# Dense projection weights laid out on the host as 96 contiguous quarters

## What is computed

```python
# block 1
u = jnp.einsum('bsd,de->bse', h, w_in[layer])          # 2048 -> 6752 columns
q, k, v, z_attn, q_idx, k_idx, w_idx, z_ssd, xbc, dt_raw = _split_cols(u, IN_WIDTHS)
...                                                    # rope, top-k attention, state space mixer
sub = jnp.einsum('bse,ed->bsd', mixed, w_out[layer])   # 2048 -> 2048
h = _layer_norm(DEEPNORM_ALPHA * h + sub, ln_g[layer], ln_b[layer])
# block 2
mod_shared = jax.nn.silu(c) @ w_mod + b_mod            # one row, 2048 -> 12288
h = rms_norm(x, norm1_g[l]) * (1.0 + scale1) + shift1
proj = h @ w_in[l]                                     # 2048 -> 2560
...                                                    # gated unit, stick-breaking attention
x = x + gate1 * (y @ w_out[l])                         # 1024 -> 2048
m = hierarchical_moe(...)                              # 32 experts, two for each token
x = x + gate2 * m
```

## Time and profile before

| | us |
|---|---|
| median of 3 runs | 1999.33 |
| lowest and highest run | 1998.57, 2000.62 |
| the profiled execution | 2000.42 |
| its span on the core | 1998.6 |

### The profile page before, as it was taken

The page is one execution under the profiler, slowest core; times in us unless marked ns, Lnnn a source line. Parts: engine busy times, 40 slices in busy tenths (PEclk is TensorE's granted clock), DMA queues, the critical chain, the costliest instruction groups (busy, mean ns, idle before and its releaser), DMA issues.

```text
span 1998.6 us, 23417 instructions
## 1 busy us (share of the span) xinstructions
PE 1860.2 (93%) x9558; PEld 1370.9 (69%) x9558; DVE 1067.0 (53%) x1551; ACT 315.2 (16%) x602; POOL 178.5 (9%) x190
## 2 busy tenths in 40 slices
PE   8999999999999999999999999999959988788876
PEld 3788988888787555888888888557845554444443
DVE  3766677544687555767774764435463332232222
ACT  0111221221300232000340122411310000000000
POOL 0000041000000000000000000000002211111211
PEclk9999999999999999999999999999969999999999
DMA  9554543222224437668545651244299999999996
GB/s 354 184 187 154 167 122 94 65 80 63 85 85 158 179 129 281 230 243 294 173 165 211 252 180 64 66 161 169 91 386 395 410 398 406 412 403 403 413 420 241
DMA packets 153225, 448.37 MB, mean 224 GB/s; under 512 B 19446, under 2 KB 118108, under 8 KB 126748
## 3 DMA queue, kind: packets, MB, share of 16 engines
q1 hardware_dynamic: 122012, 305.92, 40.2%
q0 software_dynamic: 24288, 118.32, 17.0%
q10 hardware_dynamic: 6816, 22.60, 3.2%
HBM read 440.42 MB, written 26.28 MB: 234 GB/s over the span
## 4 chain that ended last, share of the span: by engine, by line
PE 39%; DMA 20%; DVE 2%; issue 1%; ACT 0%; POOL 0%; POOLq 0%; SPq 0%; DVEq 0%; ACTq 0%
PE bank L1167 16%; DMA RW<-in_gate_up 9%; PE bank L1196 7%; DMA RG<-in_down 5%; PE bank L1106 4%; DMA RA<-xn_d,dt_ 3%; PE bank L1363 3%; PE bank L1374 2%; DMA RM<-in_down 2%; PE bank L1111 2%; DMA out<-RA,dt_ 1%; PE bank L919 1%; PE bank L992 1%; DVE RG L1958 1%; DMA RG<-in_w_mod 1%
## 5 line engine op out<-in xcount | busy, mean ns | idle before, releaser
L1167 PE MATMUL bank<-RW,RX 128*128 128x256 f32 x1344 | 300.3, 380 | 2.6 <-PE bank L1167 2.0
L1167 PEld LDWEIGHTS bank<-RW,RX 128*128 128x128 f32 x1344 | 253.7, 190 | 44.4 <-issue 10.6
L1958 DVE SCALAR_TENSOR_TENSOR RG<-RG,ccol 128x2048 f32<-128x2048 f32 x90 | 211.6, 2351 | 92.5 <-DMA RG<-in_w_mod 85.8
L1167 PE MATMUL bank<-RW,RM 128*128 128x256 f32 x1024 | 229.3, 380 | 1.5 <-PE bank L1167 0.9
L1167 PEld LDWEIGHTS bank<-RW,RM 128*128 128x128 f32 x1024 | 193.6, 190 | 31.8 <-issue 4.8
L1949 DVE TENSOR_TENSOR RW<-RW 128x2048 f32<-128x2048 f32 (+1 forms) x72 | 160.4, 2233 | 88.8 <-PE bank L1167 66.1
L1434 ACT ACTIVATE RA<-bank 128x512 f32<-128x512 f32 (+4 forms) x160 | 81.1, 540 | 559.2 <-PE bank L1167 246.9
L2879 DVE TENSOR_TENSOR RA<-RA,bank 128x128 f32<-128x128 f32 x34 | 9.8, 288 | 277.9 <-ACT RA L1918 277.7
L837 POOL DMA_DIRECT2D RG<-in_w_mod x96 | 51.4, 536 | 987.7 <-DVE RG L1958 602.0
L1111 PE MATMUL bank<-RX,RW 128*128 128x512 f32 x256 | 114.8, 593 | 2.1 <-ACT RA L1434 1.3
L1363 PE MATMUL bank<-RX,RG 128*64 128x256 f32 x768 | 90.6, 393 | 19.8 <-DMA RX<-in_gate_up 17.1
(11 more groups left out here) (294 smaller groups left out, 2462.9 us busy)
## 6 DMA issues: line engine op xcount, KB each, us to landing
RG<-in_w_mod POOLq DMA_DIRECT2D x96, 1024.0 KB, 6.2
RW<-in_w_in SPq DMA_DIRECT2D x71, 1024.0 KB, 5.4
RX<-in_gate_up SPq DMA_DIRECT2D x22, 2048.0 KB
RW<-in_gate_up SPq DMA_DIRECT2D x22, 2048.0 KB, 39.9
RG<-in_down SPq DMA_DIRECT2D x11, 2048.0 KB, 40.8
RM<-in_down SPq DMA_DIRECT2D x11, 2048.0 KB, 41.5
RM<-in_gate_up SPq DMA_DIRECT2D x10, 2048.0 KB
RH<-in_gate_up SPq DMA_DIRECT2D x10, 2048.0 KB
```

Of the source, the lines that this page charges most:

```text
L1167: ins = nc.tensor.matmul(bk[:, part], x, y, start=name not in ("M2", "M3") and k + j == 0, stop=k == half - 1, skip_group_check=True)
L1958: st.do(v.scalar_tensor_tensor(out=dst, in0=x, scalar=sc, in1=y, op0=op0, op1=op1), s, n)
```

## The change

The host cuts the weights into the 96 quarters that SP loads outside the kind "small" and stacks them as `in_quarters`, in the order of their loads, each as 128 partitions by 8 by 256. SP then reads a quarter as one run of 8 KB for each partition. The first quarter is still loaded in two halves (4 KB a partition each). An out2 quarter becomes one transfer in place of two, and its slot's count goes up by 16 in place of 32. The kind "small" is loaded as before. Nothing else in the program is different: the bytes, the slots, the order of the loads and the waits in front of them stay.

```diff
--- before.py
+++ after.py
@@ -379,13 +379,13 @@
                 return order
             return [(h, n if slots[2 * h] < slots[2 * h + 1] else 1 - n) for h, n in order]
 
-        loads, load_of, release_of = [], {}, {}
+        loads, load_of, release_of, laid_out = [], {}, {}, []
         landed = [0, 0, 0, 0]
         slots_in_turn = [0, 1, 2, 3]
         for c, ch in enumerate(chunks):
             for q in loading(c, slots_in_turn[len(loads):len(loads) + len(quarters(c))]):
                 s = slots_in_turn[len(loads)]
-                landed[s] += 32 if ch[0] in ("small", "out2") else 16
+                landed[s] += 32 if ch[0] == "small" else 16
                 load_of[c, q] = (s, landed[s])
                 loads.append((c, q))
             for q in releases(c):
@@ -716,23 +716,17 @@
                 if n >= 4:
 
                     sp.wait_ge(slot_free, n - 3)
-                if w.tensor.name == a["w_in_2"].tensor.name:
-                    rows = w.rearrange("(p k) n -> p k n", k=KD)
-                else:
+                if kind == "small":
                     rows = w.rearrange("(k p) n -> p k n", p=P)
-                if kind == "small":
                     sp.dma_start(W[:, s, :, 0:80], rows[:, 8 * h:8 * h + 8, C_KI:C_KI + 80]).then_inc(w_landed[s], 16)
                     sp.dma_start(W[:, s, :, 80:96], rows[:, 8 * h:8 * h + 8, C_DT:C_DT + 16]).then_inc(w_landed[s], 16)
-                elif kind == "out2":
-                    for part in range(2):
-                        at = 4 * (1 - part)
-                        sp.dma_start(W[:, s, 4 * part:4 * part + 4, :], rows[:, at:at + 4, col + 256 * half:col + 256 * half + 256]).then_inc(w_landed[s], 16)
                 else:
-                    at = 8 * (1 - h) if kind == "out" else 8 * h
+                    laid_out.append((w.tensor.name, kind, h, col + 256 * half))
+                    piece = a["quarters"][len(laid_out) - 1]
                     early = 4 if n == 0 else 0
                     if early:
-                        sp.dma_start(W[:, s, 0:early, :], rows[:, 0:early, col:col + 256]).then_inc(sem("x_first"), 16)
-                    sp.dma_start(W[:, s, early:, :], rows[:, at + early:at + 8, col + 256 * half:col + 256 * half + 256]).then_inc(w_landed[s], 16)
+                        sp.dma_start(W[:, s, 0:early, :], piece[:, 0:early, :]).then_inc(sem("x_first"), 16)
+                    sp.dma_start(W[:, s, early:, :], piece[:, early:, :]).then_inc(w_landed[s], 16)
                 n += 1
                 if (c, q) == (first["out2"] + 1, (0, 1)):
 
@@ -2971,6 +2965,18 @@
                         dve.wait_ge(sem(f"y_added{u}"), i * 32 + (8 * NST + 16 * (w // 2)))
                         dve.wait_ge(sem(f"wd_landed{u}"), i * 32 + 16 * (w // 2 + 1))
                         take_y(u, WDX[u][:, 0:1])
+    return laid_out
+
+
+def lay_quarter(inputs, name, kind, h, col):
+
+    w = inputs[name[3:]][0]
+    if kind == "out2":
+        return w.reshape(2, 4, P, -1)[::-1, :, :, col:col + 256].reshape(8, P, 256).transpose(1, 0, 2)
+    if name == "in_w_in_2":
+        return w.reshape(P, KD, -1)[:, 8 * h:8 * h + 8, col:col + 256]
+    at = 8 * (1 - h) if kind == "out" else 8 * h
+    return w.reshape(KD, P, -1)[at:at + 8, :, col:col + 256].transpose(1, 0, 2)
 
 
 _INS = ["x", "w_in", "w_out", "conv_w", "conv_b", "dt_bias", "a_log", "d_skip", "ssd_norm_w", "ln_g", "ln_b", "c_2",
@@ -3000,6 +3006,8 @@
     arrays["in_const"] = CONST
     args["const"] = nc.dram_tensor("in_const", CONST.shape, F32, kind="ExternalInput").ap()
     out = nc.dram_tensor("out_0", (1, S, D), F32, kind="ExternalOutput").ap()
-    program(nc, args, out)
+    args["quarters"] = nc.dram_tensor("in_quarters", (96, P, 8, 256), F32, kind="ExternalInput").ap()
+    laid_out = program(nc, args, out)
+    arrays["in_quarters"] = np.stack([lay_quarter(inputs, *piece) for piece in laid_out])
     r = run(nc, [arrays], core_ids=[0])
     return r.results[0]["out_0"]
```

## The result

| | before | changed |
|---|---|---|
| median of 9 runs each, us | 1999.46 | 2006.32 |
| lowest and highest | 1998.57, 2005.72 | 2002.14, 2012.13 |
| the profiled execution | 2000.42 | 2007.78 |
| its span | 1998.6 | 2006.1 |

The changed kernel is slower: ratio 1.0026, 95% interval 1.0016 to 1.0036, that is 3 to 7 us. The forecast was 1998.2 in a range of 1994.5 to 2002.0, with a chance of 0.09 for slower by over 0.2%.

The account below looks back on a forecast made before the run. PE was taken to bound the dense part, expert-weight transfers the expert part. Start -2.5, mod sums +1.4, rest 0 gave -1.1: 1999.3 from the profiled 2000.42, 1998.2 for the median, range 1994.5 to 2002.0.

Parts of the forecast that it names:

- What bounds the kernel: Whole kernel: dense part at PE's pace, expert part at its weights' pace; quicker quarters worth nothing on the path.
- The start: Before PE's first matmul: half quarter and x's first part land together near 7.0; gain 2.5 us, bounds 0 to 2.8.
- the bare sum: At the first matmul: 2.7 + 3.7 + 0.6 = 7.0 us, before 0.3 was taken off the gain for the fit.
- The w_mod pieces: At the mod sums at 835 and 936: pieces land later beside quarters, costing 0.7 us each, 1.4 together.
- the pair itself gets faster: Quarter and w_mod piece before a mod sum: 420 in place of 394 GB/s, piece landing at 933.7 to 934.3.
- the 1.7 us of delay: At a mod sum: piece ends with the pair's last byte, at 935.3 by today's speed, 1.7 us later.
- Rival 1: At the three mod sums: w_mod loses more than the pair gains, 1.7 at each that waits; +2.2, 2001.5 us; chance 0.17.
- Rival 2: At start and sums: nothing moves, since shares ignore run length or long runs are cut again; 1999.3 us; chance 0.14.
- rival 3: Start gives 2.8 and both mod sums' waits vanish, 2.9: clearly faster by 5.7, 1993.6 us; chance 0.14.
- its reserve: At the last mod sum: VectorE done at 1175.14, PE comes at 1178.24; 3.1 us, holding two rounds of 0.7.
- It piles up in VectorE's order: Where further pieces wait in VectorE's order: delay could pile up and the slower case pass +4 us; chance 0.09 beyond that.
- The forecast's own upper end: Whole kernel: top of the forecast's own 1996.5 to 2000, from start 1.5 to 2.8, sums 0 to 3.4 against it.

Follow-up runs that it names:

- out-old kernel: The changed kernel, but the 16 quarters of kind out loaded from w_out in runs of 1 KB as before; 1999.28 us, ratio 0.9982.

## Why the prediction was wrong, point by point

**What bounds the kernel**: right. The dense part is bound by PE, the expert part did not change, the quicker quarters gave nothing on the path, and only the start and the mod sums moved. The out-old kernel shows it for the other 80 quarters: -1.4 us, all of it from the start.

**The start**: the mechanism held, the size was off by 0.8. First matmul at 8.11 for a forecast of 7.3 (9.8 less 2.5; the bare sum said 7.0). The issues of the changed kernel, the half quarter and x's part one:

```profile
L728 SPq DMA_DIRECT2D RW<-in_quarters x1: 414/414/414, 0.9 to 0.9; - x1
...
DMA to landing us min/median/max: 7.2/7.2/7.2
```

```profile
L1430 ACTq DMA_DIRECT2D RX<-in_xt x1: 428/428/428, 0.9 to 0.9; - x1
...
DMA to landing us min/median/max: 6.6/6.6/6.6
```

They were issued together and land 0.6 apart instead of 3.7, and x's second part pays (10.5 instead of 7.6), as shares of 2 to 1 want it. The error is the rate. It was taken as 420 GB/s from 2.7 us on, from one slice. After the change the slices give 279 and 389, then 336 and 348:

```profile
3.00:4.00 1.00, 0.00 (x0) 0.00 (x0) 0.00 (x0) 0.09 (x1) 0.00 (x0) 1.00 0.72 279
4.00:5.00 1.00, 0.00 (x0) 0.00 (x0) 0.00 (x0) 0.00 (x0) 0.00 (x0) 1.00 0.99 389
```

In the other kernels whose half quarter has 4 KB runs the first matmul is at 7.3 to 8.1, and the forecast of 7.3 was met by some. It is at 7.9 to 8.1 in the four, the changed one among them, whose runs of the half quarter lie 8 KB apart, and at 7.3 to 7.5 in the three where they lie behind one another or 786 KB apart; whether the place in memory makes that half microsecond was not tried by itself. The runs of 2 KB are a test that the prediction did not have: shares of 8 to 2 let the half quarter end only with all of x, so no gain, and its first matmul was at 10.1.

**The w_mod pieces**: here it failed, in two steps. The first is the sentence "the pair itself gets faster", which brought the 1.7 us of delay down to 0.7. Its sum does not give the kernel before: at the old rate it is 928 + 5.3 + 0.6 = 933.9, and the quarter of before landed at 935.3. The sum leaves 1.4 us out, some of it the w_mod piece in front, which landed only at 929.04. Set beside the measured 933.6 of the piece, what was left out passed for speed. The two rates alone, 5.3 less 5.0, are worth 0.3 us, and 1.4 of the 1.7 would have stayed at each sum.

The pair did not get faster in the changed kernel: the quarter issued at 931.05 landed 9.2 us later, that of before 9.3, and between 935 and 937 us the two queues moved 397 GB/s, as they did in before between 930 and 932. Over all kernels the last of the pair landed 9.5 us behind the quarter's issue in the old layout (five pairs) and 9.1 with 8 KB (ten), so the gain is 0.4 in the mean, with 8.2 to 9.9 in single cases. The piece landed 9.3 and 9.1 us behind its issue instead of 6.8 and 7.3. That is 2.6 and 1.8 later, or 1.6 in the mean over the kernels with 8 KB. Rival 1 had named this place and a price of 1.7, and had a chance of 0.17.

The Trainium skill (DMA: Bandwidth & Descriptors, Queues, rings and completion order), named beside that rival, has an engine drain a whole packet, typically about 9 to 17 descriptors, before it turns to the next queue. These traces do not agree. A quarter of 128 runs on 16 engines has eight runs on each, which by that rule would go in one turn, and by an estimate from these rows the quarter would then land ahead of the piece by most of a megabyte's time, over 2 us at 394 GB/s. It lands 0.17 us ahead, and while both are under way the queues move 49 and 53 runs. Turns by about one run fit all four lengths, as shown above.

The second step is one that the sum did not have at all: it took a microsecond of PE's wait as a microsecond of time. The low clock behind the two waits cost 6.0 us, more than the waits (4.3). With delays of 1.7 at both sums and no clock the rival comes to +2.2; with 2.6 and 1.8, and 3.0 behind each, and a start of -1.67, the sum is +8.7, less the 2.3 at 1016 and plus the 1.2 behind the start, both clock that follows no layout: 7.6, measured 7.5. The trace of before held a warning that no row of the prediction shows: PE at half clock from 1013.3 to 1020.2 us, behind waits of 1.5 us and less.

**Rival 2** (nothing moves) fell at the start and at the sums, and **rival 3** (the sums' waits vanish) by the landings. The last mod sum kept its reserve, as forecast: VectorE finishes its last piece at 1181.2 and no wait of PE stands there. "It piles up in VectorE's order" was not seen: behind each sum the lag stays as it is.

**The range**: its upper end of 2002.0 was the rival's 2001.5 with a little on it. With the 3.0 us of the clock behind each sum it would have ended at 2007.5. The forecast's own upper end of 2000 does not follow from its bounds either: a start gain of 1.5 and 3.4 at the sums give 2001.2.

**A version that beats both**: the changed kernel with both sums a step later (0.9984), or with the quarters' runs apart as well (0.9979, 0.9970 to 0.9989, 1996.6 us). The two can't be told apart. Moving the sums in the kernel before gives 0.9991, so the layout's own share, once the sums are out of its way, is about the start's 1.5 to 2 us, with intervals on the ratios that are as wide.

## What to carry to other kernels

Here a transfer that got longer runs took its share from what flew beside it: before you speed up a load with a reserve of tens of microseconds, look for the load without a reserve that it meets on the engines, and ask who waits for that one. Where TensorE already waits some 2 us for something, price a further microsecond or two at two to four times their length, as the table of waits has it, since the clock may fall behind them, and read the granted clock beside the busy share, which does not show it. And where a wait depends on a place fixed by hand in an engine's order, try that place again after each change to what it waits for.

## What was not expected of the hardware

- Two queues that both have work moved about as many runs as each other, whatever the length of the runs: beside w_mod's 8 KB runs 88 to 103 with runs of 1 KB, 80 to 89 with 2 KB, 69 to 69 with 4 KB and 53 to 49 with 8 KB. Beside a transfer with 8 KB runs, one of the same size landed 1.8 us behind it with runs of 1 KB, 1.6 with 2 KB, 1.0 with 4 KB, and 0.2 ahead with 8 KB. The pair as a whole ended only 0.4 us sooner: 9.1 us in the mean with 8 KB runs, 9.5 in the old layout.
- PE's granted clock fell from 1.0 to 0.5 behind single waits in a stretch that was otherwise full: at these sums never behind 2.2 us or less, in two cases of four between 2.6 and 2.75, and always behind 2.95 or more; but a wait of 3.23 us at 948 in one kernel left it at 1.00. What is lost is what of the low clock lies behind the wait, up to 3.1 us, and 2.0 to 2.3 behind the longest waits.
- After the first matmul of an execution the matmuls ran at half speed for 3.1 to 6.2 us, differing by as much between kernels with the same first loads, while the windows print a clock of 1.00 because the record has no entry yet.
- The same transfer pair in the same program position landed anywhere from 8.0 to 9.6 us in executions of kernels that differ only in where the runs lie, in which quarters have them, or in the place of the sums. One profiled execution of each does not settle a difference of 1 us.
